# A two-block transformer kernel: where sixteen one-column sums of the modulation stand among the matmuls

## The chip, the cores and the metric

The kernel runs on one core of a Trainium2 chip. The metric is the device time of one launch in microseconds, and the median of several runs counts. Before the change it was 1209.11 us (three runs, 1209.02 to 1211.74).

## The reference

The input is 256 tokens of width 1024. A first block has two layers, each with differential attention beside a Fourier mix, a projection back, a layer norm, a SwiGLU feed-forward block and another layer norm. A second block follows with three sublayers (feed-forward, mixer, feed-forward). Each of its sublayers is modulated by a vector that comes from a conditioning input alone:

```python
mod = (silu(c) @ w_ada + b_ada).reshape(B, 3, 3, D)       # shift, scale, gate of each sublayer
u = rmsnorm(h, g) * (1 + mod[:, i, 1]) + mod[:, i, 0]     # shift and scale, before the sublayer
h = h + weight * mod[:, i, 2] * sublayer(u)               # gate, behind it
```

What is changed here belongs to `c @ w_ada`: for each of the three sublayers 3 x 1024 columns, summed over 1024 rows.

## The kernel before

All large weights come as a stream of chunks of 128 x 2048 (1 MB). SyncE loads them into three slots. ScalarE rounds a chunk to the part `w_hi` (L850), VectorE subtracts to get `w_lo` (L1193, or L1200 for half a chunk), and TensorE multiplies three products (high by high, high by low, low by high) into PSUM, at L438 and, for the gate and up projections, at L471 and L473. Activations are split in the same way: `x_full` (L858, ScalarE), then `x_hi` and `x_lo` (L1273 and L1275, VectorE, both in `x_parts`).

The modulation's product is done beside the feed-forward blocks. GpSimd loads tiles of `ada`, and VectorE multiplies and adds them (L1326) over the eight row blocks, so that `ada_acc` holds per partition a partial sum for each of 3072 columns. What is left is a sum over the 128 partitions. For the gate's 1024 columns TensorE does it with four wide products (`sum_gates`, L570). For the 2048 columns of shift and scale `sum_shifts` (L575 to L580) does it with sixteen matmuls whose stationary operand is a 128 x 128 piece of `ada_acc` and whose moving operand is one column of ones. Each writes one column of PSUM bank 1, so that the result lies as columns, one per 128 features. They are fp32, and the trace shows two passes of each. VectorE's `keep_shifts` (L1278) then adds the bias into `mods` and makes `gains` (L1280, L1284).

This happens three times, f = 0, 1, 2: at the end of the feed-forward block of layer 0, of layer 1, and of the second block's first sublayer. The vectors are read one feed-forward block later or more: f = 0 by `input_full(5)`, f = 1 by `input_full(6)`, f = 2 by `input_full(7)`.

Each of these three places is a boundary between stages with this order, written out by hand for every engine:
- PE: the last down product into banks 4 to 7 (`ffn_down(..., last_step=True)`, bank after bank); `sum_shifts`; `transposes(n)` of the normalised stream `z` into banks 2 to 5 (L528), four for every tile of z as it lands; then the first chunk's products as the input tiles are ready. Behind boundary f = 0 and f = 2 that is `token_projection` into banks 0 and 1 (L438), behind f = 1 `split_projection` (L471).
- DVE: for each of the four banks the residual (L1231, or L1247 and L1251 in the second block, each counting `summed`), then statistics, the normalised tiles `z` (L1240 or L1266), the rest of the first chunk's split, `keep_shifts`, and the input split. At f = 1 it normalises twice, since the first block's last layer norm is followed by the second block's RMS norm.
- ACT: chunk splits, then `input_full` as soon as `transposed` counts.

`pe.wait_ge(ada_kept, ...)` keeps PE from writing bank 1 before `keep_shifts` has read it. In the code before it stands between the transposes and the products at all three boundaries (L682, L746, and ahead of the mixer's first `token_projection`). `fourier_tables` writes banks 6 and 7 four projections' worth of work into a layer, `values2` writes them in the mixer.

Of the kernel before, what the change touches and what calls it, by code (L numbers as in the profile page):

```python
# [30 lines left out]
P = 128  # L31
# [19 lines left out]
MODS = 3 * KT  # L51
SHIFT_SCALE = 2 * KT
# [25 lines left out]
def fused_blocks(nc, x, stream, ada, w_f, layer_params, common_params, rows, consts32, out):  # L78
    with ExitStack() as ctx:
# [10 lines left out]
        h = sb("h", [P, 2, D])  # L90
# [15 lines left out]
        mods = sb("mods", [P, 72])  # L106
# [55 lines left out]
        ones = c32[:, ONES:ONES + P]  # L162
# [267 lines left out]
        def _(pe):  # L430
# [46 lines left out]
            def token_projection(t, j, banks, c, before):  # L477

                pe.wait_ge(lo_ready, 3 * t + (j + 1))
                wh, wl = chunk(w_hi, j % SLOTS, 4), chunk(w_lo, j % SLOTS, 4)  # L480
                for i in range(4):
                    k = 4 * c + i
                    before(k)
                    for m in range(2):
                        cols = slice(m * P, (m + 1) * P)
                        last = passes(banks[m][:, :], wh[:, i, :], wl[:, i, :], x_hi[:, k, cols], x_lo[:, k, cols],
                                      True, k == 0, k == KT - 1)
                last.then_inc(chunk_done, 1)
# [29 lines left out]
            def input_tile(n):  # L518

                return lambda k: pe.wait_ge(x_ready, 8 * back(n) + (k + 1))  # L520

            def transposes(n):

                for i, b in enumerate((0, 2, 1, 3) if n < 2 * DEPTH else range(4)):
                    m, c = b // 2, b % 2
                    pe.wait_ge(z_ready, 4 * back(n) + i + 1)
                    for k in range(4 * c, 4 * c + 4):
                        last = nc.tensor.transpose(XT[k // 2][:, k % 2 * S + m * P:k % 2 * S + (m + 1) * P],  # L528
                                                   z[:, m, k * P:(k + 1) * P], ident)
                        if m == 1 and k % 2 == 1:  # L530
                            last.then_inc(transposed, 1)

            def ffn_down(t, j, step, first=False, last_step=False):

                pe.wait_ge(hid_ready, step + 1)
                hh, hl = (hid_hi2, hid_lo2) if last_step else (hid_hi, hid_lo)
                to_residual(t, j, hh, hl, (0, 1), first, last_step)

            def ffn(t, j, f, n_in, with_ada):

                def gate_up(t, j, i):
                    pe.wait_ge(gate_ready, FT * f + i)
                    split_projection(t, j, GATE)
                    pe.wait_ge(up_ready, FT * f + i)
                    split_projection(t, j + 1, UP)

                split_projection(t, j, GATE, before=input_tile(n_in))
                split_projection(t, j + 1, UP)
                gate_up(t, j + 2, 1)
                ffn_down(t, j + 4, FT * f, first=True)  # L550
                with pe.Fori(0, FT - 3) as i:
                    gate_up(t + i, j + 5, i + 2)
                    ffn_down(t + i, j + 7, FT * f + i + 1)
                gate_up(t + (FT - 3), j + 5, FT - 1)
                ffn_down(t + (FT - 3), j + 7, FT * f + (FT - 2))
                if with_ada:
                    sum_gates(f)
                ffn_down(t, j + 3 * FT - 1, FT * f + (FT - 1), last_step=True)
                if with_ada:
                    sum_shifts(f)  # L560

            def sum_gates(f):

# [8 lines left out]
                                                start=i == 0, stop=i == 1)  # L572
                last.then_inc(gates_reduced, 1)

            def sum_shifts(f):  # L575

                for q in range(SHIFT_SCALE):
                    last = nc.tensor.matmul(B[1][:, q:q + 1], ada_acc[:, q * P:(q + 1) * P], ones[:, 0:1],  # L578
                                            start=True, stop=True, skip_group_check=True)
                last.then_inc(shifts_reduced, 1)  # L580

            def warm_up(count):

# [8 lines left out]
            for l in range(DEPTH):  # L592
# [37 lines left out]
                def fourier_tables():  # L630

                    pe.wait_ge(consts_landed, 16)
                    pe.wait_ge(wf_landed, 16 * DEPTH)
                    for c, part in ((0, cos_c), (1, neg_sin_c)):
                        nc.tensor.matmul(B[6 + c][:, :], part, wf[l][:, :, :].rearrange("p g n -> p (g n)"),
                                         start=True, stop=True).then_inc(tables_done, 1)
# [42 lines left out]
                    pe.wait_ge(gate_sums_kept, 2 * l)  # L679
                transposes(2 * l)  # L680
                if l > 0:
                    pe.wait_ge(ada_kept, l)  # L682
                for c in range(2):
                    token_projection(t, V0 + c, B[0:2], c, input_tile(2 * l))
                fourier_tables()
                for c in range(2):
                    token_projection(t, U0 + c, B[2:4], c, input_tile(2 * l))
# [55 lines left out]

            pe.wait_ge(gate_sums_kept, 4)
            transposes(5)
            pe.wait_ge(ada_kept, 2)  # L746
            ffn(FFN1_T, 0, 2, 5, True)
            pe.wait_ge(gate_sums_kept, 6)
            transposes(6)

            t = MIX_T
            EV = 8 * DEPTH
# [22 lines left out]

            def values2(h):
                pe.wait_ge(a2_ready, h + 1)
                if h % 2 == 0 and h >= 4:
                    pe.wait_ge(o2_ready, h // 2 - 1)
                r = VD * (h % 2)  # L780
                out = B[6 + h // 2 % 2][r:r + VD, :]
                nc.tensor.matmul(out[:, 0:S], v_s[:, 0, h * VD:(h + 1) * VD], log_a[:, h % 4, 0:S], start=True,
                                 stop=False, skip_group_check=True)
                nc.tensor.matmul(out[:, P:S], v_s[:, 1, h * VD:(h + 1) * VD], log_a[:, h % 4, S:S + P], start=False,
                                 stop=True, skip_group_check=True).then_inc(o2_done, 1)
# [403 lines left out]
        def _(dve):  # L1189
            def split(t, j):  # L1190

                dve.wait_ge(hi_ready, 3 * t + (j + 1))
                nc.vector.tensor_tensor(w_lo[j % SLOTS][:, :], raw[j % SLOTS][:, :],  # L1193
                                        w_hi[j % SLOTS][:, :].bitcast(F32), ALU.subtract).then_inc(lo_ready, 1)
# [82 lines left out]

            def keep_shifts(f):  # L1278
                dve.wait_ge(shifts_reduced, f + 1)
                nc.vector.tensor_tensor(mods[:, MODS * f:MODS * f + SHIFT_SCALE], B[1][:, 0:SHIFT_SCALE],  # L1280
                                        cp[:, B_ADA + MODS * f:B_ADA + MODS * f + SHIFT_SCALE], ALU.add)\
                    .then_inc(ada_kept, 1)
                dve.wait_ge(ada_kept, f + 1)
                nc.vector.scalar_tensor_tensor(gains[:, f, :], mods[:, MODS * f + KT:MODS * f + 2 * KT], 1.0,  # L1284
                                               cp[:, NORM_G + KT * f:NORM_G + KT * f + KT], ALU.add, ALU.mult)\
                    .then_inc(mods_step, 1)

            def keep_gates(f):
                dve.wait_ge(gate_rows_landed, 48)
                for c, kept in ((0, gate_rest), (1, up_sum)):  # L1290
                    dve.wait_ge(gate_sums_kept, 2 * f + c + 1)
                    row = gate_rows[:, f, c * HALF:(c + 1) * HALF]
                    nc.vector.tensor_tensor(row, kept, row, ALU.add).then_inc(gates_kept, 1)
# [78 lines left out]
            for l in range(DEPTH):  # L1372
# [3 lines left out]
                if l == 0:  # L1376
                    dve.wait_ge(first_half_hi, 1)
                    nc.vector.tensor_tensor(w_lo[0][:, 0:CH // 2], raw[0][:, 0:CH // 2],
                                            w_hi[0][:, 0:CH // 2].bitcast(F32), ALU.subtract)
                    dve.wait_ge(hi_ready, 1)  # L1380
                    nc.vector.tensor_tensor(w_lo[0][:, CH // 2:], raw[0][:, CH // 2:],
                                            w_hi[0][:, CH // 2:].bitcast(F32), ALU.subtract).then_inc(lo_ready, 1)
                else:
                    split_half(t, 0, 1)
                    keep_shifts(l - 1)
                input_split(2 * l, range(0, KT // 2))
                split(t, 1)
                input_split(2 * l, range(KT // 2, KT))
                if l > 0:
                    keep_gates(l - 1)  # L1390
                split(t, 2)
                split(t, 3)
# [141 lines left out]
            sum_of_squares(5, 0)  # L1534
            rms_scaled(5)
            split_half(FFN1_T, 0, 1)
            keep_shifts(1)
            input_split(5)
            split(FFN1_T, 1)
            keep_gates(1)  # L1540
            split(FFN1_T, 2)
            ffn(FFN1_T, 0, 2, True)
            gated_residual(6, 3 * MIX_T)
            rms_scaled(6)
            split_half(MIX_T, 0, 1)
            keep_shifts(2)
            input_split(6, range(0, KT // 2))
            split(MIX_T, 1)
            input_split(6, range(KT // 2, KT))
            keep_gates(2)  # L1550

            t = MIX_T
# [243 lines left out]
```

## Time and profile before

| | |
|---|---|
| median of three runs | 1209.11 us (1209.02 to 1211.74) |
| the profiled execution | 1212.48 us, its span 1210.8 us |
| PE busy | 1171.8 us, 97% of the span |
| DVE busy | 864.4 us, 71% |
| ACT busy | 611.0 us, 50% |
| mean granted TensorE clock | 0.983 of 2.4 GHz |
| all sums of L578 | 96 passes, 165 to 353 ns each, 309.6 to 819 us |

PE is the engine of TensorE's matmuls and PEld its weight loads, which overlap. A pass is recorded once on each. The granted clock is 1.00 at 2.4 GHz and 0.50 at 1.2 GHz. A recorded matmul's time overlaps with its neighbours', so the pace is read from starts.

### The profile page before, as it was taken

How to read it: one execution, taken by the hardware profiler on the slowest of the kernel's cores; microseconds unless marked ns; L12 is line 12 of the kernel's file. 1: busy time of each engine (PE TensorE's matmuls, PEld its weight loads, DVE VectorE, ACT ScalarE, POOL GpSimd, SP SyncE). 2: the span in 40 equal slices, each digit the busy share in tenths (PEclk: the TensorE clock that was granted, in tenths of full speed). 3: DMA queues.
4: the chain of work that ended last, by engine and by line, in shares of the span. 5: the costliest groups of instructions: out<-in, count | busy, mean ns of one | idle time of the engine just before them, and what ended most of it. 6: DMA issues, size and time to landing. Idle time of an engine off the chain costs nothing.

```text
span 1210.8 us, 17757 instructions
## 1 busy us (share of the span) xinstructions
PE 1171.8 (97%) x6642; PEld 1008.8 (83%) x6642; DVE 864.4 (71%) x1130; ACT 611.0 (50%) x745; POOL 102.8 (8%) x99
## 2 busy tenths in 40 slices
PE   8998999999999899999979999999999999999997
PEld 7987888888897788888868888878989987888886
DVE  6576878888857687888796788876477477655555
ACT  5573644444557464444444444544795445544443
POOL 2400600000130060000010000000000000000000
PEclk9999999999899999999989999998999998999999
DMA  9622567775452267777536677644424553555540
GB/s 361 238 70 105 206 265 275 297 292 201 151 188 70 105 214 267 271 303 280 213 145 216 240 288 272 263 169 174 175 90 154 174 179 136 202 179 183 198 173 35
DMA packets 34992, 242.62 MB, mean 200 GB/s; under 512 B 3809, under 2 KB 5233, under 8 KB 8449
## 3 DMA queue, kind: packets, MB, share of 16 engines
q1 hardware_dynamic: 28992, 196.56, 43.8%
q0 software_dynamic: 5520, 45.17, 10.3%
q8 instruction: 33, 0.54, 0.2%
q10 hardware_dynamic: 432, 0.24, 0.1%
q14 instruction: 15, 0.11, 0.0%
HBM read 240.90 MB, written 1.05 MB: 200 GB/s over the span
## 4 chain that ended last, share of the span: by engine, by line
PE 82%; DVE 8%; ACT 5%; issue 3%; DMA 0%; POOL 0%; DVEq 0%; SPq 0%; ACTq 0%
PE bank L438 39%; PE bank L471 25%; PE bank L473 13%; ACT w_hi L850 2%; DVE work L1326 1%; PE bank L625 1%; DVE small L1218 1%; PE bank L528 1%; PE bank L578 1%; PE bank L602 1%; DVE w_lo L1193 1%; DVE h L1231 1%; PE bank L615 1%; DVE h L1251 0%; PE bank L643 0%
## 5 line engine op out<-in xcount | busy, mean ns | idle before, releaser
L1193 DVE TENSOR_TENSOR w_lo<-raw,w_hi 128x2048 fp32r<-128x2048 f32 x178 | 414.2, 2329 | 143.7 <-ACT w_hi L850 143.5
L471 PE MATMUL bank<-x_parts,w_hi 128*128 128x512 f32 x1408 | 501.6, 400 | 2.4 <-DVE x_parts L1275 2.1
L473 PE MATMUL bank<-x_parts,w_lo 128*128 128x256 f32 x1408 | 396.3, 281 | 0.0
L850 ACT ACTIVATE w_hi<-raw 128x2048 fp32r<-128x2048 f32 x183 | 349.1, 1908 | 45.6 <-PE bank L438 39.7
L471 PEld LDWEIGHTS bank<-x_parts,w_hi 128*128 128x128 f32 x1408 | 265.9, 189 | 69.9 <-issue 3.4
L473 PEld LDWEIGHTS bank<-x_parts,w_lo 128*128 128x128 f32 x1408 | 267.2, 190 | 1.4
L438 PE MATMUL bank<-x_parts,w_hi 128*128 128x256 f32 x832 | 153.0, 286 | 0.7 <-ACT work L1109 0.7
L438 PE MATMUL bank<-w_hi,hid_hi 128*128 128x512 f32 x352 | 139.3, 396 | 2.8 <-DVE hid_lo L1314 2.8
L438 PE MATMUL bank<-w_lo,hid_hi 128*128 128x512 f32 x352 | 139.0, 395 | 0.0
L438 PE MATMUL bank<-w_hi,hid_lo 128*128 128x512 f32 x352 | 138.8, 394 | 0.0
L438 PEld LDWEIGHTS bank<-x_parts,w_hi 128*128 128x128 f32 x832 | 129.3, 191 | 3.8 <-issue 2.0
L438 PE MATMUL bank<-x_parts,w_lo 128*128 128x256 f32 x416 | 117.5, 283 | 0.0
L1326 DVE SCALAR_TENSOR_TENSOR work<-work,c_act 128x384 f32 x168 | 104.0, 619 | 5.9
L890 ACT ACTIVATE hid_hi<-work 128x512 fp32r<-128x512 f32 x44 | 27.8, 631 | 128.5 <-PE bank L438 114.7
L874 ACT ACTIVATE work<-bank 128x512 f32<-128x512 f32 x44 | 26.3, 598 | 126.2 <-PE bank L473 122.6
L438 PEld LDWEIGHTS bank<-w_hi,hid_hi 128*128 128x128 f32 x352 | 66.0, 187 | 20.0 <-DVE hid_lo L1314 4.1
L438 PEld LDWEIGHTS bank<-x_parts,w_lo 128*128 128x128 f32 x416 | 79.6, 191 | 0.0
L438 PEld LDWEIGHTS bank<-w_hi,hid_lo 128*128 128x128 f32 x352 | 66.0, 187 | 16.0
L438 PEld LDWEIGHTS bank<-w_lo,hid_hi 128*128 128x128 f32 x352 | 66.0, 188 | 14.1
L438 PE MATMUL bank<-w_hi,x_parts 128*128 128x512 f32 x224 | 74.0, 408 | 2.3 <-DVE x_parts L1275 1.5
L1314 DVE TENSOR_TENSOR hid_lo<-work,hid_hi 128x512 fp32r<-128x512 f32 x44 | 32.7, 744 | 59.6 <-ACT hid_hi L890 59.6
L356 POOL TENSOR_TENSOR small<-small 128x1 f32<-128x1 f32 x18 | 11.8, 654 | 532.6 <-DVE small L1257 421.5
(176 smaller groups left out, 1251.3 us busy)
## 6 DMA issues: line engine op xcount, KB each, us to landing
raw<-stream SPq DMA_DIRECT2D x183, 1024.0 KB, 4.8
work<-ada POOLq DMA_DIRECT2D x24, 1536.0 KB, 6.7
gain_rows<-rows POOLq DMA_DIRECT2D x11, 512.0 KB, 5.5
gate_rows<-rows POOLq DMA_DIRECT2D x3, 512.0 KB, 17.5
h<-x SPq DMA_DIRECT2D x4, 256.0 KB, 4.7
raw<-stream SPq DMA_DIRECT2D x2, 512.0 KB, 6.8
out<-z SPq DMA_DIRECT2D x4, 256.0 KB, 2.1
c<-consts SPq DMA_DIRECT2D x1, 962.0 KB, 13.9
```

Of the source, the lines that this page charges most:

```text
L438: last = nc.tensor.matmul(out, stationary, moving, start=start and i == 0, stop=stop and i == 2, skip_group_check=True)
L471: nc.tensor.matmul(pair[:, n, :], wh[:, k, cols], x_parts[:, k, :, :].rearrange("p a n -> p (a n)"), start=k == 0, stop=False, skip_group_ ...
L473: last = nc.tensor.matmul(pair[:, n, 0:S], wl[:, k, cols], x_hi[:, k, :], start=False, stop=k == KT - 1, skip_group_check=True)
L528: last = nc.tensor.transpose(XT[k // 2][:, k % 2 * S + m * P:k % 2 * S + (m + 1) * P], z[:, m, k * P:(k + 1) * P], ident)
L578: last = nc.tensor.matmul(B[1][:, q:q + 1], ada_acc[:, q * P:(q + 1) * P], ones[:, 0:1], start=True, stop=True, skip_group_check=True)
L602: last = nc.tensor.matmul(SCORES[u][:, m * S:(m + 1) * S], qT[r:r + HD, p, m * P:(m + 1) * P], kT[r:r + HD, p, :], start=True, stop=True, ...
L850: nc.scalar.activation(w_hi[j % SLOTS][:, :], raw[j % SLOTS][:, :], ACT.Copy).then_inc(hi_ready, 1)
L874: nc.scalar.activation(gate_rest.rearrange("p (a n) -> p a n", a=2), GATE[:, :, S:2 * S], ACT.Copy)\
L890: nc.scalar.activation(out[:, :, :].rearrange("p k n -> p (k n)"), hidden, ACT.Copy)\
L1193: nc.vector.tensor_tensor(w_lo[j % SLOTS][:, :], raw[j % SLOTS][:, :], w_hi[j % SLOTS][:, :].bitcast(F32), ALU.subtract).then_inc(lo_ready, 1)
L1314: nc.vector.tensor_tensor(lo[:, :, :].rearrange("p k n -> p (k n)"), hidden, hi[:, :, :].rearrange("p k n -> p (k n)").bitcast(F32), ALU.s ...
L1326: nc.vector.scalar_tensor_tensor(acc, ada_raw[:, k, :], c_act[:, k:k + 1], acc, ALU.mult, ALU.add).then_inc(ada_step, 1)
```

## The change

The sums go to bank 6, which is the third bank of the residual stream, and are split into two parts. Ten of the sixteen stand where all stood, in front of the transposes; ahead of them PE waits until VectorE has summed the third bank (`summed` at 7, 15 or 19). Six stand behind the transposes, in front of the first products. `keep_shifts` reads bank 6, and on VectorE it moves behind the input split and the next chunk's split. The waits on `ada_kept` move to where bank 6 is written next: `fourier_tables`, the first down product of the feed-forward block (`n_in == 5`), and `values2(0)`.

```diff
+                if n_in == 5:
+                    pe.wait_ge(ada_kept, 2)
                 ffn_down(t, j + 4, FT * f, first=True)
...
                 if with_ada:
-                    sum_shifts(f)
+                    sum_shifts(f, SUMS_BEFORE)
...
-            def sum_shifts(f):
-
-                for q in range(SHIFT_SCALE):
-                    last = nc.tensor.matmul(B[1][:, q:q + 1], ada_acc[:, q * P:(q + 1) * P], ones[:, 0:1],
+            def sum_shifts(f, part):
+
+
+                if part[0] == 0:
+                    pe.wait_ge(summed, (7, 15, 19)[f])
+                for q in part:
+                    last = nc.tensor.matmul(B[6][:, q:q + 1], ada_acc[:, q * P:(q + 1) * P], ones[:, 0:1],
                                             start=True, stop=True, skip_group_check=True)
-                last.then_inc(shifts_reduced, 1)
+                if part[-1] == SHIFT_SCALE - 1:
+                    last.then_inc(shifts_reduced, 1)
+
+            SUMS_BEFORE, SUMS_BEHIND = range(0, 10), range(10, SHIFT_SCALE)
...
                 transposes(2 * l)
                 if l > 0:
-                    pe.wait_ge(ada_kept, l)
+                    sum_shifts(l - 1, SUMS_BEHIND)
                 for c in range(2):
                     token_projection(t, V0 + c, B[0:2], c, input_tile(2 * l))
+                if l > 0:
+                    pe.wait_ge(ada_kept, l)
                 fourier_tables()
...
             transposes(5)
-            pe.wait_ge(ada_kept, 2)
+            sum_shifts(1, SUMS_BEHIND)
             ffn(FFN1_T, 0, 2, 5, True)
             pe.wait_ge(gate_sums_kept, 6)
             transposes(6)
+            sum_shifts(2, SUMS_BEHIND)
...
                 pe.wait_ge(a2_ready, h + 1)
+                if h == 0:
+                    pe.wait_ge(ada_kept, 3)
...
-                nc.vector.tensor_tensor(mods[:, MODS * f:MODS * f + SHIFT_SCALE], B[1][:, 0:SHIFT_SCALE],
+                nc.vector.tensor_tensor(mods[:, MODS * f:MODS * f + SHIFT_SCALE], B[6][:, 0:SHIFT_SCALE],
...
                     split_half(t, 0, 1)
-                    keep_shifts(l - 1)
                 input_split(2 * l, range(0, KT // 2))
                 split(t, 1)
                 input_split(2 * l, range(KT // 2, KT))
                 if l > 0:
+                    keep_shifts(l - 1)
                     keep_gates(l - 1)
...
             split_half(FFN1_T, 0, 1)
-            keep_shifts(1)
             input_split(5)
             split(FFN1_T, 1)
+            keep_shifts(1)
             keep_gates(1)
...
             split_half(MIX_T, 0, 1)
-            keep_shifts(2)
             input_split(6, range(0, KT // 2))
             split(MIX_T, 1)
             input_split(6, range(KT // 2, KT))
+            keep_shifts(2)
             keep_gates(2)
```

## Rows read from the trace of the kernel before

**Rows 1.** Page: busy us, share of the span, instructions of each engine.
```profile
PE 1171.8 (97%) x6642; PEld 1008.8 (83%) x6642; DVE 864.4 (71%) x1130; ACT 611.0 (50%) x745; POOL 102.8 (8%) x99
```

**Rows 2.** Chain of waits: start us, us, what; the first two boundaries.
```profile
310.03 4.21 PE bank L578 x32
...
620.52 0.88 DVE z L1266 x2
```

**Rows 3.** Timeline, layer 0 to 1: start, us, engine, line, operation, count, [idle before].
```profile
309.38 0.68 DVE L1231 SCALAR_TENSOR_TENSOR h<-h,bank 128x512 f32<-128x512 f32 x1
...
309.64 4.51 PEld L578 LDWEIGHTS bank<-c,work 128*128 128x128 f32 x32
...
312.45 0.54 DVE L1240 TENSOR_SCALAR z<-h,small 128x512 f32<-128x512 f32 x1
...
313.43 1.46 DVE L1240 TENSOR_SCALAR z<-h,small 128x512 f32<-128x512 f32 x3 [0.44 <-POOL small L356]
313.89 3.46 PEld L528 LDWEIGHTS bank<-c,z 128*128 128x128 f32 x16
...
315.94 0.17 DVE L1280 TENSOR_TENSOR mods<-bank,cp 128x16 f32<-128x16 f32 x1
...
316.58 0.43 DVE L1275 TENSOR_TENSOR x_parts<-x_full,x_parts 128x256 fp32r<-128x256 f32 x1
...
317.33 0.34 PEld L438 LDWEIGHTS bank<-w_hi,x_parts 128*128 128x128 f32 x1
```

**Rows 4.** Windows: stretch, length, busy us PE PEld DVE ACT POOL, PEclk, DMA.
```profile
312.50:313.00 0.50, 0.50 (x4) 0.50 (x5) 0.49 (x2) 0.00 (x0) 0.39 (x1) 0.55 0.00 0
...
319.00:319.50 0.50, 0.50 (x3) 0.40 (x2) 0.50 (x2) 0.40 (x1) 0.00 (x0) 0.62 1.08 459
...
626.50:627.00 0.50, 0.50 (x4) 0.45 (x3) 0.47 (x2) 0.42 (x1) 0.00 (x0) 0.92 1.04 442
...
824.50:825.00 0.50, 0.50 (x3) 0.38 (x3) 0.47 (x3) 0.50 (x2) 0.00 (x0) 0.95 0.67 279
```

**Rows 5.** Timeline, layer 1 to the second block.
```profile
611.54 3.77 PEld L578 LDWEIGHTS bank<-c,work 128*128 128x128 f32 x32
...
613.92 0.68 DVE L1231 SCALAR_TENSOR_TENSOR h<-h,bank 128x512 f32<-128x512 f32 x1
...
621.12 3.28 PEld L528 LDWEIGHTS bank<-c,z 128*128 128x128 f32 x16 [5.81 <-issue]
...
625.27 0.28 PEld L471 LDWEIGHTS bank<-x_parts,w_hi 128*128 128x128 f32 x1 [0.88 <-issue]
...
632.06 0.50 PE L471 MATMUL bank<-x_parts,w_hi 128*128 128x512 f32 x1 [0.37 <-DVE w_lo L1193]
```

**Rows 6.** Timeline, first feed-forward block to the mixer.
```profile
814.79 4.49 PEld L578 LDWEIGHTS bank<-c,work 128*128 128x128 f32 x32
814.82 0.69 DVE L1251 TENSOR_TENSOR h<-h,z 128x512 f32<-128x512 f32 x1
...
816.88 0.88 DVE L1266 TENSOR_SCALAR z<-h,small 128x512 f32<-128x512 f32 x2
...
818.63 0.88 DVE L1266 TENSOR_SCALAR z<-h,small 128x512 f32<-128x512 f32 x2 [0.66 <-POOL small L356]
819.02 3.46 PEld L528 LDWEIGHTS bank<-c,z 128*128 128x128 f32 x16
...
823.17 0.28 PEld L438 LDWEIGHTS bank<-w_hi,x_parts 128*128 128x128 f32 x1 [0.69 <-issue]
```

**Rows 7.** Layer 1's inner boundary: a window, as rows 4, and PE's timeline.
```profile
417.00:418.00 1.00, 0.00 (x0) 0.00 (x0) 0.96 (x3) 0.00 (x0) 0.00 (x0) 1.00 0.00 0
...
420.32 1.57 PE L528 MATMUL bank<-c,z 128*128 128x128 f32 x12 [0.34 <-DVE z L1240]
```

**Rows 8.** Mixer to the last feed-forward block: PE's timeline and a window.
```profile
1014.89 0.76 PE L471 MATMUL bank<-x_parts,w_hi 128*128 128x512 f32 x1 [0.32 <-DVE x_parts L1275]
...
1019.00:1020.00 1.00, 1.00 (x7) 0.87 (x6) 1.00 (x2) 0.19 (x1) 0.00 (x0) 0.94 0.00 0
```

## The prediction

> **What bounds the kernel now.** I read the engine table first: TensorE (PE) is busy 97% of the span, VectorE (DVE) 71%, ScalarE 50% [rows 1]. So a change counts where it moves PE's next full-rate product, and hardly elsewhere. Then the chain of waits, for the lines the change touches. The one-column sums (L578) stand on it with 4.21 us at the boundary from layer 0 to layer 1 (A, near 310 us), and with a second such row at the boundary from the first feed-forward block to the mixer (C, near 815 us). At the boundary in between (B, near 611 us) the chain is on VectorE, which normalises twice there [rows 2]. Last I read the timeline of each boundary and the granted clock in half-microsecond slices.
>
> The three boundaries differ in how much of PE's time is free:
> - A: PE has no gap at all. The sums' weight loads start at 309.64 as the last down product ends, the transposes' at 313.89, the first projection's at 317.33 [rows 3].
> - C: the same up to the transposes (814.79, 819.02). The projection's first load is at 823.17, after a wait of some 0.3 us for the split input [rows 6].
> - B: the sums run from 611.54 to about 615.3, and the transposes start at 621.12 only, when z is there. These sums lie wholly in a wait of VectorE and cost nothing. Behind the transposes (last load ends 621.12 + 3.28 = 624.40) there are 0.87 us until the first product at 625.27 [rows 5].
>
> At A the granted clock falls from 1.00 to 0.50 (2.4 to 1.2 GHz) at 312.55, some 2.5 us after the last 512-column product. It comes back at 319.3, 626.55 and 824.55 at the three boundaries (a slice with 0.62, 0.92 or 0.95 holds the step), that is 2.0, 1.3 and 1.35 us into the projection [rows 4]. At C it is down by the transposes as well: their loads take the same 3.46 us [rows 3, 6]. So the sums begin at the high clock, and whatever is issued behind the transposes runs at the low one.
>
> **The change part by part.**
>
> *Price of a sum.* Each is two passes (x32 for sixteen). At the high clock all of B's took 3.77 us of loads for 32 passes, less the last load's tail: 0.115 us a pass, 0.23 a sum [rows 5]. At A, 2.9 us at this pace (309.64 to 312.55) are 25 passes, which leaves 7 for the 1.34 us up to 313.89: 0.19 to 0.20 us a pass at the low clock, 0.4 a sum [rows 3, 4]. The transposes, one pass each, are 3.46 us for 16 there, 0.21 each. Six sums behind the transposes therefore cost 12 x 0.2 = 2.4 us, with 1.4 us (high clock) as their other bound. A page would have it otherwise: the row shows that a one-column pass takes as long as a weight load, however short its stream is [rows 3, 5]. The Trainium skill, "TensorE: Matmul & The Clock Gate", Part 1, says that matmuls of any small width start no closer than about 25 ns; by that alone six sums would be an estimated 0.3 us and vanish in the wait behind the transposes. That is rival 3; the rows speak against it.
>
> *The new wait.* The sums go to bank 6, which VectorE reads as the residual's third bank. PE's queue is in order, so ten sums and all transposes stand behind this wait. At A that read ends at 309.38 + 0.68 = 310.06, at C (the wait is on the addition into h) at 814.82 + 0.69 = 815.51 [rows 3, 6]. PE starts some 0.15 us after VectorE's end (621.12 after 620.52 + 0.44) [rows 5]. So the sums begin at 310.21 and 815.66 and not at 309.64 and 814.79. At B they begin at 614.75 (613.92 + 0.68 + 0.15) and end by 617.1, four microseconds before z: free.
>
> *A, PE's sequence.* Ten sums: 310.21 + 20 x 0.115 = 312.5. The first z tile ends at 312.99, so transposes start at 313.14 and not 313.89; the second lands at 313.92 (the three from 313.43 take 1.46), so the second four start at 314.07, and the last twelve need 12 x 0.206: 316.54 [rows 3]. Then 2.4 us of sums: the projection starts at 318.9 and not at 317.33: **+1.6 us**. VectorE gets rid of 0.37 us ahead of the input split (keep_shifts from 315.94: 0.17 us, a gap, and a second one like it), and the first input tile, ready at 317.01, would be ready at 316.7; PE is now later than that, so this buys nothing [rows 3].
>
> *B.* The transposes stand where they were. The sums run 624.4 to 626.8, the first product is 1.5 us late. VectorE's chain (input split, then the next chunk's split) let PE wait 0.37 us at 632.06 for the second chunk [rows 5]; that wait swallows so much, so **+1.2 us** (VectorE's own chain gets shorter by keep_shifts, which only moves the end of this wait forward).
>
> *C.* Ten sums end at 815.66 + 2.3 = 817.9; the first two z tiles are there (816.88 + 0.88 = 817.76), so eight transposes run to 819.6; the next tile ended at 819.07, eight more to 821.2. Sums to 823.6, against 823.17: **+0.45 us** [rows 6].
>
> *The clock behind them.* The full-rate products now start later and have one-column sums ahead of them, where before transposes stood ahead. The products ran at the low clock for 2.0, 1.3 and 1.35 us. At the last boundary of the kernel (near 1013 us), with 2 us of transposes and a short gap in front, the clock came back 4.2 us into them (1014.89 to 1019.1) [rows 8]. I take these as bounds: nothing more than before, or 4.2 us at each. Sums behind the transposes are thin work, as the fall at A and C during sums shows, so I take a value in the upper half: 3.1 us at each on average, 1.6 more than now, at half speed 0.8 us lost each, **+2.4 us** (0 to 4.0; below nothing, if the clock returned at once each time: the 4.65 us at half speed, -2.3).
>
> *The rest at nothing.* keep_shifts goes behind the input split: the readers of what it writes are gains and mods of a stage one feed-forward block later. The moved waits on ada_kept come before the tables (A, two chunks of products into the layer), before the first down product (B) and before values2 (C), all long after VectorE gets there. If VectorE were late by its whole split of 2.3 us, they would still be covered: PE is at work on two chunks of 5 us and more each before it asks. No DMA is moved or added.
>
> *Sum*: 1.6 + 1.2 + 0.45 + 2.4 = 5.65, taken as 5.7 us. The rows come from an execution of 1212.5 us (span 1210.8), 3.4 us above the median of 1209.1; I put the difference onto the median: **1214.8 us**.
>
> **Rivals.**
> 1. *The clock term is not there.* It returns as soon after the products' start as now: 1.6 + 1.2 + 0.45 = +3.3, 1212.4 us (A and C weigh most, where PE has no gap). With sums at the high clock it is less still. For it: before, the return came within 2.0 us at all three. Against: the bare return took 4.2 us at the fourth [rows 8].
> 2. *Faster: the clock stays up at A and C.* The front is shorter and the transposes follow sooner. For it: at the layer's inner boundary (417 to 420 us) the clock stayed at 1.00 through a wait and the transposes took 1.57/12 = 0.13 us each [rows 7]. Then at A the transposes end at 314.07 + 12 x 0.115 = 315.45, sums at 316.8 (-0.5) and the products lose their 2.0 us of low clock (-1.0). At C transposes start at 817.92, are done at 820.1, sums at 821.5 (-1.65, -0.65). B keeps +1.2 and +0.8. Total -1.8: 1207.3 us. It decides only if both falls disappear. Against: the same thin work follows the last product, with a wait of 0.5 us ahead of it.
> 3. *The six sums vanish in the wait for the input tiles.* The front gains are then left: A starts when the tile is ready (316.7, -0.6), B -0.35, C at 821.4 (-1.8): -2.75, 1206.4 us. It needs a pass below 0.05 us; the rows show 0.115 at the best.
>
> **How the numbers follow.** Forecast (all terms, clock lost to some degree) 0.72, rival 1 0.19, rival 2 0.05, rival 3 0.02, something unseen 0.02. A measurement tells about 0.3% or 3.6 us: rival 1 lies just within it, and a small clock term does as well. Faster 0.06, within 0.3% 0.2, slower 0.74. The forecast's own range is 1212.8 (low clock a little longer) to 1216.4 (4.2 us at all three: 3.3 + 4.0 = +7.3). The range that is to hold 8 in 10 goes down to 1210.8, for sums nearer the high clock (-1.0 at a boundary) or an early return, and up to 1217.5.
>
> **What would show it.** In the profile after: at A, L578's ten sums start near 310.2 and its six near 316.5 with passes of 0.2 us, and the first projection load is 1.3 to 1.9 us later after the last down product than now; at B the gap behind the transposes is full and PE's wait for the second chunk is gone; at C the projection is 0.3 to 0.7 us later. The clock stays at 0.50 for over 2 us of the products. I am wrong if the transposes after the change run at 1.00, if a sum behind them costs under 0.2 us, or if PE waits after them for x_parts.

## The result, and the profile after

The changed kernel took 1219.98 us (median of five runs, 1218.96 to 1222.47) against 1209.02 us for the kernel before beside it: a ratio of 1.0086 (95% interval 1.0072 to 1.010), slower by some 10.4 us. The forecast was 1214.8 us with a range up to 1217.5. The direction held; the time did not, and most of the loss has a reason that the forecast had at nothing. A second measurement gave 1220.73 against 1210.56, ratio 1.0082 (1.0066 to 1.0098).

The page of the changed kernel (busy us, share, instructions) has PE at nearly the same work as [rows 1]:

```profile
PE 1174.8 (96%) x6642; PEld 1010.8 (83%) x6642; DVE 864.8 (71%) x1130; ACT 611.1 (50%) x745; POOL 102.6 (8%) x99
```

Its span is 1218.0 us, 7.2 more than before. PE's busy time grew by only 3.0 us, so PE must also stand somewhere. The view of the waits, of PE from 820 to 840 us (who waited for whom: us in total, times, longest), names the place:

```profile
PE bank L438 <- DVE mods L1293: 4.8, 1, 4.8
```

L1293 is `keep_shifts`. PE's own timeline at that place, and VectorE's (start, us, engine, line, operation):

```profile
822.50 2.69 PEld L583 LDWEIGHTS bank<-c,work 128*128 128x128 f32 x12
...
822.67 0.42 DVE L1288 TENSOR_TENSOR x_parts<-x_full,x_parts 128x256 fp32r<-128x256 f32 x1
...
825.00 2.29 DVE L1206 TENSOR_TENSOR w_lo<-raw,w_hi 128x2048 fp32r<-128x2048 f32 x1
...
829.86 0.17 DVE L1293 TENSOR_TENSOR mods<-bank,cp 128x16 f32<-128x16 f32 x1
...
830.08 0.80 PE L438 MATMUL bank<-w_hi,x_parts 128*128 128x512 f32 x1 [4.80 <-DVE mods L1293]
```

The first input tile was ready at 823.09 (822.67 + 0.42) and the sums were through by 825.1, yet the projection began at 830.08. In between VectorE does the rest of the first four input tiles, the split of the next chunk (825.00), four more input tiles, and then keep_shifts (829.86). PE waits for that because the line `pe.wait_ge(ada_kept, 3)` ahead of the mixer's first `token_projection` **is still there**. The section on the change says that the wait moves to `values2(0)`; that is not so. The change adds a second wait there, and takes the old one away at A and B, but at C its diff has no minus line for it. In the kernel before this wait was free: keep_shifts came right behind the first split. The change moved keep_shifts behind the second split, and left the wait in front. Nothing needs it there any more, as the sums no longer write bank 1.

A, B and C are the three boundaries, as in the prediction. At A the steps came out in this profile as they had been put [rows 3]. PE's loads in the changed kernel:

```profile
310.13 2.52 PEld L583 LDWEIGHTS bank<-c,work 128*128 128x128 f32 x20 [0.51 <-DVE h L1244]
...
313.13 0.72 PEld L528 LDWEIGHTS bank<-c,z 128*128 128x128 f32 x4 [0.48 <-issue]
...
314.05 2.42 PEld L528 LDWEIGHTS bank<-c,z 128*128 128x128 f32 x12 [0.21 <-DVE z L1253]
...
316.46 2.68 PEld L583 LDWEIGHTS bank<-c,work 128*128 128x128 f32 x12
...
319.02 0.33 PEld L438 LDWEIGHTS bank<-w_hi,x_parts 128*128 128x128 f32 x1
```

The projection starts 1.7 us later than at 317.33. The six sums last 2.56 us at the low clock, 0.21 us a pass. At B they met the high clock in this execution (1.42 us of loads for the same twelve passes) and cost nothing: from the first of the gates' wide products ahead of B to the first of those ahead of C it is 203.05 us (605.92 to 808.97), and was 203.25 (603.95 to 807.20). Five other profiles, shown further down, say that this was chance.

### The profile page after: what moved, and what is told of

Read it like the earlier page. It is cut to its first block, busy times and chain, and to the rows that moved or that the text cites. A ratio compares the mean times of both kernels' runs of the same rounds, so it can differ in the third digit from the quotient of the medians.

```text
span 1218.0 us, 17758 instructions
## 1 busy us (share of the span) xinstructions
PE 1174.8 (96%) x6642; PEld 1010.8 (83%) x6642; DVE 864.8 (71%) x1130; ACT 611.1 (50%) x745; POOL 102.6 (8%) x99
## 4 chain that ended last, share of the span: by engine, by line
PE 80%; DVE 11%; ACT 5%; issue 3%; DMA 0%; POOL 0%; DVEq 0%; SPq 0%; ACTq 0%
PE bank L438 38%; PE bank L471 25%; PE bank L473 12%; ACT w_hi L863 2%; DVE work L1339 1%; DVE small L1231 1%; DVE w_lo L1206 1%; PE bank L633 1%; DVE x_parts L1288 1%; DVE h L1244 1%; PE bank L610 1%; DVE h L1264 1%; PE bank L528 1%; DVE z L1260 1%; PE bank L623 1%
## 5 line engine op out<-in xcount | busy, mean ns | idle before, releaser
L438 PEld LDWEIGHTS bank<-w_hi,x_parts 128*128 128x128 f32 x224 | 44.8, 200 | 17.4 <-DVE mods L1293 4.9
```

The costliest lines, as they stand in the source:

```text
L438: last = nc.tensor.matmul(out, stationary, moving, start=start and i == 0, stop=stop and i == 2, skip_group_check=True)
```

## The experiments

All times are medians beside runs of the kernel before on the same chip, with the ratio's 95% interval; differences in us are worked out from the ratio where nothing else is said. Each run has a short name (e1 and so on), which stands with its edit. Lines of kernels left out of an edit are marked by `...`. The kernel before itself spread from 1205.3 to 1213.4 us over these runs.

### The left-over wait taken out

The changed kernel without the wait, e1:

```diff
-            pe.wait_ge(ada_kept, 3)
             for c in range(2):
                 token_projection(t, c, B[0:2], c, input_tile(6))
```

> The changed kernel with one line less: the wait on ada_kept (3) ahead of the mixer's first projection, which the change left standing although bank 1 is no longer written by the sums; a second wait of the same kind was added in values2. Theory W (left-over wait): in the changed kernel PE stood from 825.1 to 830.1 us for keep_shifts, which now comes behind the input split. Without the line these 5.0 us go, and about 1 us of low clock with them: some 1214 us against 1220 for the changed kernel, and +4 to +6 against the kernel before, which is what the prediction's own terms (5.7) say. Rival S (the sums and the new wait in front cost it all, the 5 us cover other waits): it stays at 1218 to 1220.

Measured: 1212.45 against 1211.32, ratio 1.0013 (0.9998 to 1.0029). Of a loss of 0.86% (0.72 to 1.0) 0.13% (-0.02 to 0.29) is left, 1.6 us. So the line costs about 8.8 us (10.4 less 1.6, measured beside two sets of runs): the 5 us of standing, and more. Rival S is out. The sums' own part is smaller than the prediction's 5.7 us and than the +4 to +6 written here; the upper end of the interval is 3.5 us.

The trace of this run tells one part of why. At C, in its timeline (start, us, what):

```profile
818.20 2.31 PEld L583 LDWEIGHTS bank<-c,work 128*128 128x128 f32 x20 [0.82 <-DVE h L1263]
...
821.80 0.86 PEld L528 LDWEIGHTS bank<-c,z 128*128 128x128 f32 x8 [0.52 <-DVE z L1278]
...
822.63 1.42 PEld L583 LDWEIGHTS bank<-c,work 128*128 128x128 f32 x12
...
824.06 0.19 PEld L438 LDWEIGHTS bank<-w_hi,x_parts 128*128 128x128 f32 x1
```

and in its windows (length; PE, PEld, DVE, ACT, POOL busy; the number behind POOL's is the granted clock):

```profile
820.00:821.00 1.00, 1.00 (x11) 1.00 (x11) 0.60 (x2) 0.35 (x2) 0.32 (x1) 1.00 0.00 0
...
824.00:825.00 1.00, 1.00 (x6) 0.85 (x6) 0.93 (x4) 1.00 (x3) 0.00 (x0) 1.00 0.88 131
```

The clock stayed at 1.00 through C in this execution: second eight transposes and six sums at half the price, and the projection 5.9 us behind the third bank's addition and not 7.7 as before (815.51 to 823.17). At A (sums from 308.11, projection 317.01) it was low as predicted. At B it was low as well, and the products began 1.7 us later behind the transposes' start than before (622.12 to 627.94 is 5.82 us, against 4.15).

### The late keep_shifts alone

```diff
             split_half(MIX_T, 0, 1)
-            keep_shifts(2)
...
             input_split(6, range(KT // 2, KT))
+            keep_shifts(2)
             keep_gates(2)
```

This is e2, on the kernel before, with the sums untouched.

> The kernel before, with only keep_shifts(2) moved behind the input split, as the change has it; sums, bank and PE's waits are as before. Theory W: the mixer's first projection then starts when keep_shifts is through, near 830 us and not at 823.2: +6.9 us and up to +1 us of low clock, some 1216 to 1217 us. Rival S: no change, 1209, because nothing of the sums was moved.

Measured: 1219.64 against 1211.32, ratio 1.0064 (1.0042 to 1.0086), +7.8 us. One moved call costs three quarters of what the whole change does. PE's line at C:

```profile
830.40 0.80 PE L438 MATMUL bank<-w_hi,x_parts 128*128 128x512 f32 x1 [7.16 <-DVE mods L1280]
```

### Boundaries A and B only, and C only

In e4 A and B are changed, and at C all sixteen sums stand in front, in bank 1, with keep_shifts early. Part of its edit against the changed kernel:

```diff
-                    sum_shifts(f, SUMS_BEFORE)
+                    sum_shifts(f, SUMS_BEFORE if f < 2 else range(SHIFT_SCALE))
...
-            sum_shifts(2, SUMS_BEHIND)
...
```

> The change at boundaries A (layer 0 to 1) and B (layer 1 to the second block) only; C (to the mixer) has all sixteen sums in front, bank 1 and the early keep_shifts. The prediction's terms give 1.6 + 1.2 + 1.6 (clock) = +4.4 us, 1213.4. The two traces read at the next boundaries give +2.0 for A and -0.2 for B, 1210.8; in that trace B met the high clock during its six sums. Rival S: nearly the whole loss of 11 us is here and at C in equal parts, so +7, 1216.

Measured: 1212.02 against 1211.32, ratio 1.0009 (0.9996 to 1.0023), +1.1 us (-0.5 to 2.8 by the interval). The forecast's 4.4 us is outside.

And the reverse, e9: C changed without the left-over wait, A and B as before. Part of its edit against the kernel before:

```diff
-                    sum_shifts(f)
+                    sum_shifts(f, SUMS_BEFORE if f == 2 else range(SHIFT_SCALE))
...
-            pe.wait_ge(ada_kept, 3)
...
```

> The change at boundary C alone, left-over wait gone; A and B as before. The prediction's terms give +0.45 and +0.8 for the clock, 1.2 us over the kernel before. The trace of e1 had the granted clock at 1.00 all through C and its projection started 5.9 us after the third bank's sum, against 7.6 before: if that is the rule (the transposes come 0.8 to 1.4 us sooner and keep the clock up) it is 2 to 3.5 us faster than before. If it is chance, one run in some, the mean is between, near 0.

Measured: 1209.5 against 1210.82, ratio 0.9994 (0.9981 to 1.0007), -0.7 us (-2.3 to 0.8). So C alone, without the left-over wait, shows no cost and no gain that can be told; in its profile the clock fell for 3.4 us, half of what it did before at C.

### The six sums behind the transposes left out

```diff
-                for q in part:
+                for q in (part if part[0] == 0 else ()):
...
```

This is e7, on e1. It doesn't compute six of the sixteen columns of shift and scale, and serves only to price them.

> As e1 (left-over wait gone), and the six sums behind the transposes are left out, so that six of the sixteen columns of shift and scale aren't computed. This prices them with the clock that they cost. If they stand on PE's path as the prediction says: 2.2 us at A, 0.3 to 1.5 at B, 2 at C, and 1 to 2.4 us of clock, so 5.5 to 8 us under e1, about 1207 us, 1 to 3 us under the kernel before. If they lie beside the wait for the input tiles (rival 3 of the prediction): within 1 us of e1.

Measured: 1207.85 against 1211.32, ratio 0.9985 (0.997 to 1.000). Against e1 that is 0.28%, 3.4 us for the eighteen sums of the three boundaries, where 5.5 to 8 were expected. In its profile the projection at A starts at 314.62, with sums from 307.94 on: 6.7 us, against 8.9 in e1. So the six cost 2.2 us at A, as put. At B they cost 1.8 us by the same two profiles: from the gates' products ahead of B to those ahead of C it is 203.06 us in e7 (601.06 to 804.12) and 204.87 in e1 (604.95 to 809.82). What is missing is at C: from there to the end e1 needs 0.8 us less than e7 in these profiles, and its clock had stayed up.

### All sixteen in front

```diff
-            SUMS_BEFORE, SUMS_BEHIND = range(0, 10), range(10, SHIFT_SCALE)
+            SUMS_BEFORE, SUMS_BEHIND = range(0, SHIFT_SCALE), ()
...
```

This is e3, on e1: bank 6, the new wait in front, and keep_shifts behind the input split.

> As e1 (left-over wait gone, bank 6), with all sixteen sums in front of the transposes behind the new wait, none behind. Prediction's terms: the wait costs 0.5 us at A and 0.9 at C and nothing at B, less about 0.3 at each for keep_shifts out of the way of the input split, so about +1 us against before, and 0.5 us under e1. If the clock is what counts (thin work right ahead of the projection), e1 is 2 us and more over this one.

Measured: 1210.98 against 1210.82, ratio 1.000 (0.9988 to 1.0012). The new wait, the new bank and the later keep_shifts together are free within 1.5 us. Against e1, which has six of the sums behind the transposes, e3 is 0.13% faster, but the two intervals overlap: that the split in two parts gains or costs anything by the time is not shown.

### The place of keep_shifts in VectorE's queue, with the wait left in

The changed kernel, with keep_shifts(2) right behind the first four input tiles (e10), and behind keep_gates(2) (e11). With them ran the changed kernel itself, unedited (e0).

```diff
             input_split(6, range(0, KT // 2))
+            keep_shifts(2)                       # e10
             split(MIX_T, 1)
             input_split(6, range(KT // 2, KT))
-            keep_shifts(2)                       # e10 and e11
             keep_gates(2)
+            keep_shifts(2)                       # e11
```

> The changed kernel itself, beside the next two on one chip. Theory W gives +7 to +10 us against the kernel before (the wait 5 to 6, the moved sums 1 to 2, the low clock behind the wait 1 to 2).

> The changed kernel, left-over wait and all, with keep_shifts(2) ahead of the split of the mixer's second chunk and the last four input tiles, so 4.9 us sooner in VectorE's queue. Theory W: VectorE is there at 825.0, just as PE's sums end (825.1), keep_shifts is through by 825.5, and PE waits some 0.4 us and not 4.8. So 4.5 to 6 us less than the changed kernel, within 1 us of e1, where the wait was taken out. If the place of the sums or the bank is what costs: no change.

> The changed kernel with keep_shifts(2) behind keep_gates(2), whose two additions last 1.29 us. Theory W: PE's wait grows from 4.8 to 6.1 us and the time by 1.3 us, 1.5 with a longer low clock. The rival, that the wait lies beside something else: no change. The spread of single runs is as large as this; the wait in the profile decides.

| | us | before | ratio | PE's wait for keep_shifts in the profile |
|---|---|---|---|---|
| changed kernel | 1220.73 | 1210.56 | 1.0082 (1.0066 to 1.0098) | 6.8 us (4.8 in the first profile) |
| two steps sooner | 1213.66 | 1210.56 | 1.0034 (1.0018 to 1.0049) | 0.3 us |
| one step later | 1220.32 | 1210.56 | 1.0078 (1.0060 to 1.0096) | 6.0 us |

PE's first product of the mixer in the three profiles, in this order:

```profile
832.57 0.29 PEld L438 LDWEIGHTS bank<-w_hi,x_parts 128*128 128x128 f32 x1 [6.88 <-DVE mods L1293]
```
```profile
822.38 0.79 PE L438 MATMUL bank<-w_hi,x_parts 128*128 128x512 f32 x1 [0.32 <-DVE mods L1293]
```
```profile
829.68 0.29 PEld L438 LDWEIGHTS bank<-w_hi,x_parts 128*128 128x128 f32 x1 [6.11 <-DVE mods L1293]
```

Moving the call forward in VectorE's queue takes 5.8 us off by the ratios (7.1 by the medians), with the wait in place. The step of 1.3 us backward can't be told in the time. In the profile the length of the wait misleads: it was to grow from 4.8 to 6.1 us and is 6.0, but the changed kernel's own wait is 4.8 in one profile and 6.8 in the next, as the sums ahead of it ran at the high clock there and were through sooner (1.42 us of loads from 824.27 in the second profile, 2.69 from 822.50 in the first). Its end is the better measure. From VectorE's addition of the third bank to the mixer's first product it is 12.79 us and 12.78 us in the changed kernel's two profiles (817.29 to 830.08, 819.79 to 832.57), and 13.98 in e11 (815.70 to 829.68): the step backward moves the projection by 1.2 us, where 1.3 was put. In e10 it is 7.93 (814.45 to 822.38). The sooner version stays 0.2% over e1 in ratio; whether that is real is open.

### A version that beats both

PE has a gap of about 1 us ahead of each last down product, where it waits for hid_lo (0.9 us ahead of C in the profile of the kernel before). Bank 1 is free there, as `sum_gates` has waited for its readers. In e5 the kernel before has four sums in that gap and twelve in front of the transposes, keep_shifts and its wait as before:

```diff
                 if with_ada:
                     sum_gates(f)
+                    sum_shifts(f, range(0, 4))
                 ffn_down(t, j + 3 * FT - 1, FT * f + (FT - 1), last_step=True)
                 if with_ada:
-                    sum_shifts(f)
+                    sum_shifts(f, range(4, SHIFT_SCALE))
...
```

> The kernel before with bank 1, where the first four sums stand between the gate's wide products and the last down product, in PE's wait of 0.9 to 1.4 us for hid_lo, and twelve in front of the transposes. Twelve last 2.8 us and are through before the first z tile is there: the transposes start 0.75 us sooner at A and 1.1 to 1.3 sooner at C, B stays. At A VectorE's input tile holds the projection, so -0.2 to -0.4; at C -1.0 to -1.3. Together 1.2 to 1.7 us faster than before; if the clock stays up more often by it, 3. If the four do not fit the wait they delay the last down product: no gain.

Measured: 1208.37 against 1210.82, ratio 0.9985 (0.9975 to 0.9995), 1.8 us faster than before and, by the ratios, some 12 us faster than the changed kernel. In its profile at C:

```profile
807.20 1.09 PEld L581 LDWEIGHTS bank<-c,work 128*128 128x128 f32 x8
...
813.98 2.88 PEld L581 LDWEIGHTS bank<-c,work 128*128 128x128 f32 x24
...
816.70 1.51 PEld L528 LDWEIGHTS bank<-c,z 128*128 128x128 f32 x8
...
818.37 1.57 PEld L528 LDWEIGHTS bank<-c,z 128*128 128x128 f32 x8 [0.17 <-DVE z L1270]
...
820.91 0.19 PEld L438 LDWEIGHTS bank<-w_hi,x_parts 128*128 128x128 f32 x1 [0.98 <-DVE mods L1284]
```

From the first sum in front to the projection it is 6.9 us, against 8.4 before (814.79 to 823.17 [rows 6]), and at A 7.4 (309.17 to 316.60) against 7.7. The four sums take 1.09 us of loads in the gap and delay nothing: from the gates' products to the sums in front it is 7.59 us with them (806.39 to 813.98) as without (807.20 to 814.79). But e5 also ran less at the low clock than the kernel before beside it (the table below), and the trace of one execution doesn't separate the two; that the gain comes from the shorter front is argued, not shown.

Run e6 moves keep_shifts into VectorE's wait for GpSimd as well, between the normalised tiles, shown for f = 2:

```diff
-            rms_scaled(6)
+            rms_scaled(6, lambda: keep_shifts(2))
             split_half(MIX_T, 0, 1)
-            keep_shifts(2)
...
```

> e5, with keep_shifts moved into VectorE's wait for GpSimd's root between the normalised tiles (0.44 us at A, 0.66 at B and C), so that it no longer stands ahead of the input split. 0.3 us less at A and B each, nothing at C, against e5: 1.8 to 2.3 us faster than before. If the twelve sums are not through by then VectorE waits for them and z is late: slower than e5.

Measured: 1208.3 against 1210.82, ratio 0.9985 (0.9975 to 0.9996). It is as fast as e5 within what these runs tell; the 0.6 us put between them is too small for them.

## Why the prediction was wrong

**The step that failed is "The rest at nothing".** It said that the moved waits on ada_kept come before the tables (A), the first down product (B) and values2 (C), "all long after VectorE gets there". At C the wait did not move. It was doubled. The text of the code before said where the wait stood, and the diff shows no line that takes it away, so this could be read without any profile. With it the price follows from the kernel before: the first input tile is ready near 823 us, then come three more input tiles, a split of 2.3 us and four more tiles, some 7 us ahead of keep_shifts. That is what e2 gives (+7.8 us), and e1 takes it away again (8.8 of the 10.4 us). The last sentence of the prediction ("wrong ... if PE waits after them for x_parts") looked for a wait, but for another one.

**The clock has a share in the price of this wait.** The changed kernel's first product of the mixer comes 12.8 us behind the addition of the third bank, and 5.9 and 7.0 us behind it in the profiles of e1 and e9, which lack the wait: 5.8 to 6.9 us of delay. In the changed kernel's windows the clock was 0.50 from the transposes through the wait and came back at 834.4, 4.3 us into the projection:

```profile
829.00:830.00 1.00, 0.00 (x0) 0.00 (x0) 0.96 (x4) 0.00 (x0) 0.00 (x0) 0.50 0.66 270
...
834.00:835.00 1.00, 1.00 (x5) 0.77 (x4) 0.00 (x0) 0.00 (x0) 0.00 (x0) 0.80 0.38 49
```

In e1 and e9 the whole projection ran at 1.00. At half the speed 4.3 us lose 2.2. Together that is an estimate of 8.0 to 9.0 us from three profiles, and 8.8 were measured.

The mean granted clock c of each run gives the time at the low clock, 2 x (1 - c) x span:

| | runs | low clock, mean us |
|---|---|---|
| before (beside e1, e2, e4, e7) | 29 | 42.1 |
| e1, wait out | 12 | 42.4 |
| e2, late keep_shifts alone | 5 | 49.7 |
| e4, A and B only | 11 | 44.7 |
| e7, six left out | 12 | 39.2 |
| before (beside e3, e5, e6, e9) | 35 | 41.4 |
| e9, C only, without the wait | 12 | 37.7 |
| e5, four in the gap | 12 | 37.0 |
| before (beside e0) | 17 | 43.8 |
| changed, first and second measurement | 5, 5 | 50.2, 51.7 |

(All rows hold the low stretch at the end of a run, where PE is done: 3.6 to 5.6 us in the profiles.) The wait brings some 8 us more at the low clock (e2 has 7.6 more, the changed kernel's second measurement 7.9 more than the kernel before beside it), but only the part of it in which PE has dense work costs time. Over the 81 runs of the kernel before, a microsecond more at the low clock goes with 0.19 us of span (correlation 0.67), not with half.

**The price of a sum was right, and PE's sequence at A in half of the profiles**: 0.115 us a pass at the high clock, 0.21 at the low one (put at 0.2), the first sum at 310.13 (put at 310.21), and the projection +1.7 us (put at +1.6) in both profiles of the changed kernel and in e1. In e4, e10 and e11 the clock was high for nearly all of the sums behind A's transposes, and it is -0.5 to +0.6 us, taken from the addition of the third bank. Rival 3, with sums that vanish, is out: e7 prices them at 3.4 us.

**B came as put.** Taken from the gates' wide products ahead of B to those ahead of C, the stretch that holds only B:

| profiles | us | low clock around B |
|---|---|---|
| nothing behind B's transposes: before, e2, e3, e5, e6, e7, e9 | 202.9 to 203.3 | 10.2 us in each |
| six sums there: e0, e1, e4, e10, e11 | 204.8 to 206.0 | 13.7 us in four, 17.1 in e4 |
| six sums there: the changed kernel's first profile | 203.05 | 10.2 us |

So against the 203.25 us of the kernel before the six sums cost 1.5 to 2.7 us in five of six profiles, where 1.2 and 0.8 for the clock were put.

**A second term was mis-sized: C and its clock.** The clock term, +2.4 us, meant 4.8 us more at the low clock (1.6 at each boundary). The runs of e1 show 0.3 more, with a standard error of 1.6. By the same table A and B bring 2.6 more (e4, put at 3.2) and C alone 3.7 less (e9, put at 1.6 more), each with a standard error of a little over 2. Where C is changed and nothing stands in the way, the profiles show no low stretch (e1) or 3.4 us (e9), and 6.8 us where C is as it was (before, e4). I had taken three clock returns of one execution as what the kernel does. So the forecast without the left-over wait, +5.7 us, is too high: +1.6 us were measured in e1 (-0.2 to 3.5), +1.1 for A and B together in e4 (put at 4.4) and -0.7 for C in e9 (put at 1.2). One sign that the prediction had named for being wrong is there as well: in e1's profile the transposes at C ran at 1.00. Of the single boundaries only B is settled by the profiles; the division of the rest between order of work and chance of the clock stays open.

Rival 1 (no clock term, +3.3 us, 1212.4) is within e1's interval, but that is luck. Its condition was that the clock returns as soon as before behind the products' start. At A it took 3.4 to 3.7 us in three profiles (before: 2.0), and in three the clock was back before the products or had never fallen, and at B it took 3.0 to 5.7 us in five (before: 1.3); the sum comes out near because C had less. Rival 2 (the clock stays up at A and C) is what e1's profile shows at C; e10's shows it at A; no profile has both.

## What to carry to other kernels

When a change moves the instruction that fulfils a wait, list every wait on that semaphore in the code that results, and not only the lines that the diff names; a wait that was free turns into one of the whole distance that its releaser moved. PE, where it stood in front of a dense stretch, paid twice here: once for standing, and once for 4.3 us at the low clock behind it, against 1.4 before. Small work is best tried where its engine waits already and the data is complete: the version with four sums in a gap was 1.8 us faster (0.6 to 3.0), and shifting six behind the transposes gained nothing.

## What the hardware showed that I had not expected

- The low-clock time of the same kernel differs from run to run. In the two profiles of the unedited changed kernel it is 10.2 and 13.7 us around B, and within layer 1, near 384 us, none and 6.8 us. Over 81 runs of the kernel before it is 24 to 56 us, and it goes with the spread of these runs, 8 us, by a correlation of 0.67. With 12 runs beside 29 the interval reaches some 1.9 us to either side, so that terms of 1 to 2 us stay unresolved.
- The same work does not always let the clock fall. In e1 it stood at 1.00 at C through 2.3 us of one-column sums, 2.3 us of transposes with a gap, and 1.4 us of sums again. In the changed kernel's first profile it fell to 0.50 at 820.75, 3.5 us behind the third bank's addition, with the same order and pace up to there.
